# x loaded a second time with its axes exchanged and normed in place, scores scaled at the drain, and block 2's norm, the choices and the expert rows put in another order

## The chip, the core and the metric

One core of one Trainium2 chip runs the whole kernel. The metric is device time in microseconds (us). One profiled execution of the kernel before is read; its engines are PE (TensorE, with PEld for its weight loads), DVE (VectorE), ACT (ScalarE), POOL (GpSimd, which only issues indirect DMAs here) and SP (SyncE, which only issues DMAs).

## The reference

One layer on x, 512 tokens by 1024 features, all float32. What matters, cut down:

```python
hn = rmsnorm(x, mix_norm_w)                 # x * rsqrt(mean(x^2)) * w
z, xbc, dt_raw, q, k, v = split(hn @ w_in)
y = concat(ssd_branch(z, xbc, dt_raw), diff_attention(q, k, v))
x = x + y @ w_out
xn = rmsnorm(x, ffn_norm_w)
# PEER, 8 heads: scores of 2 x 128 keys, top 16 of each half, top 16 of their sums
h = gelu(xn . peer_u[idx]);  x = x + sum((g * h) * peer_v[idx])   # 128 experts a token, of 16384
```

In the attention a head has two score maps (queries and keys of 64 features, scale 64 ** -0.5), a softmax of each, and the value product of the first less lambda times the second.

## The kernel before, in words

Tokens lie in four blocks of 128. Blocks 0 and 1 are half 0, blocks 2 and 3 are half 1. `T8[:, half]` holds the operand of the projections with features on partitions: 8 chunks of 128 features by 256 tokens.

`work_order()` (L93) writes one list of steps, `ORDER`. PE, ACT and DVE each walk it and do their part of every step, in that order, so an engine that waits holds back all its later steps. Semaphores join them.

**Start.** SP loads x (four blocks), constants, `WDT`, `ROWS`, then the weight tiles of `w_in`, 2 MB each in two halves. ACT and DVE square and sum x (L877, L1108), `inverse_mean` and a root give the factor, L1115 writes the normed block to `Y`, PE turns it with 8 transposes a block (L597, 32 in all), and DVE drains the banks into `T8` with the norm's weight (L1101, two a block). Steps: x is one block of 128 channels of the convolution's input (8 logical products, L627), dt the 8 columns of dt (L743, both halves of the tokens), cv a convolution, acs, z, q, k, v, S1 to S3 (the SSD branch) follow.

**Attention**, blocks 0 and 1 (maps i = 0 to 7) and then blocks 2 and 3 (i = 8 to 15), written by `attention()`. Step A: PE scores (L701), DVE maximum and its scaled negative (L1372, L1375), ACT exponentials (L968). c: DVE joins the two maps (L1382). B: PE turns the map (L711), ACT copies it (L976). C: values (L723) into bank 2. N and n2: norm of a block, on DVE and ACT (L1387 to L1398, L985 to L991). T turns the normed block, R0 and R1 multiply it with `w_out` (L635), F and U norm and turn the sum, W and K (L807) give queries and scores of the keys. Between the maps lie fill products and, on DVE, rows.

**Expert layer.** Half 0 fetches its experts' rows: for a token's 128 experts one row of u (`ru`, L1431, 1.22 us of DVE) and one of v (`rv`, L1436, 1.28 us), each an indirect DMA of 512 KB issued by POOL (L1481) into one of 5 to 13 places (`RING`, and spaces in `BIG` while these are free). Half 1 goes densely over all 128 tiles of `u_t` and of v: step gl (L824) is one tile of u_t, 64 of them before the one-hot steps begin; r and y are DVE's choices of the top 16; sel turns the choices (PE L830), ACT copies them to `KT3` (L1056, L1059), oh builds one-hot matrices from them (DVE L1340, ACT), og multiplies them (PE L843), gm and gw multiply the gates into `HBUF` (L1452, L1456). The second 64 turns of the loop at L192 hold oh, gm, gl, og, gw and two or three rows each. Then come 128 tiles of v (L849) on PE and the rest of the rows on DVE, and `fin` (L1464) adds the two and stores.

The order of choices and rows among the first 64 gl steps is written by a cost loop: an item is put before gl j+1 while the costs spent are under a due time,

```python
while w < len(work) and spent < 3.44 * (j + 1) - 4:      # L186
```

where 3.44 us is one gl step. Scores of half 0's block 1 are stored to DRAM (`away`, L527) between the key load (L525) and the last tiles of `w_q`.

Of the kernel before, what the change touches and what calls it, by code (L numbers as in the profile page):

```python
# [92 lines left out]
def work_order():  # L93
# [87 lines left out]
    work += [first] + rows(2) + on("sel", 0) + rows(2) + on("oh", 0) + [second] + rows(3) + on("oh", 1) + [keys]  # L181
    work += rows(1) + on("ws", 3)
    spent, w = 0.0, 0
    for j in range(FIRSTJ):
        o += on("gl", j) if j else []
        while w < len(work) and spent < 3.44 * (j + 1) - 4:  # L186
            o.append(work[w])
            spent += cost[work[w][0]]
            w += 1
    o += work[w:]  # L190
    g = 0
    for k, j in enumerate(range(FIRSTJ, NKEY)):  # L192
        if 0 < g < NGRP - 1:
            o += on("oh", g + 1)
        if k >= 3:
# [6 lines left out]
        o += rows(2 + (k % 4 == 0))  # L202
# [11 lines left out]
def block_program(nc, x, w_in, w_out, w_q, keys_t, u, u_t, v, rows, ffn_w, cols, consts, out, away, x_kept):  # L214
    ctx = ExitStack()
    with ctx:
# [82 lines left out]
        LT = TMP[:, 0, 0:QKD]  # L299
        WC = sb("WC", [P, 8])  # L300
# [43 lines left out]
        ld_x = [sem(f"ld_x{i}") for i in range(NB)]  # L344
        ld_id, ld_par, ld_fw, ld_keys, ones_set = (sem(n) for n in ("ld_id", "ld_par", "ld_fw", "ld_keys", "ones_set"))
# [17 lines left out]
        chosen, g_raw, g_exp, idx_ready = (sem(n) for n in ("chosen", "g_raw", "g_exp", "idx_ready"))  # L363
        t_late, dense_keys, n_half, f_half = sem("t_late"), sem("dense_keys"), sem("n_half"), sem("f_half")
# [105 lines left out]
        def y_count(kind, b):  # L470
            return b + 1 if kind == 0 else NB + 1 + NORMS[("NF"[kind - 1], b)]

        def turned(b):

            return (t_done, 2 * NB + TURNS[("T", b)] + 1), (t_late, TURNS[("T", b)] + 1)

        def t_count(kind, b):
            return 2 * b if kind == 0 else 2 * NB + 2 * TURNS[("T", b)]
# [24 lines left out]
        def _(sp):  # L503
            for b in range(NB):
                sp.dma_start(X[:, b, :], x[b * P:(b + 1) * P, :]).then_inc(ld_x[b], 16)
                if b == 1:
                    sp.dma_start(CONST[:], consts[:, 0:2 * P]).then_inc(ld_id, 16)
            sp.dma_start(COLS[:], cols).then_inc(ld_par, 16)
# [4 lines left out]
            for n, (mat, c0) in enumerate(tiles):  # L513
                if n == 2:
                    sp.wait_ge(t_full, 2 * NB)
# [14 lines left out]
                for half in range(2):  # L530
                    s = (2 * n + half) % NHALFW
# [991 lines left out]
```

## Time and profile before

| | us |
|---|---|
| three runs | 1433.91, 1436.22, 1436.32 (median 1436.22) |
| the profiled execution | 1435.16 |
| its span, first to last instruction | 1433.4 |
| PE busy | 1376.7 (96%) |
| DVE busy | 1107.8 (77%) |
| ACT / POOL busy | 400.2 / 615.9 |
| moved by DMA | 466.12 MB, 325 GB/s in the mean |
| mean granted TensorE clock | 0.992 |

1.8 us of the execution's time lie outside the span. A busy PE is an engine with a matrix product in flight. Matrix products in float32 are two records each.

### The profile page before, as it was taken

How to read it: one execution, taken by the hardware profiler on the slowest of the kernel's cores; microseconds unless marked ns; L12 is line 12 of the kernel's file. 1: busy time of each engine (PE TensorE's matmuls, PEld its weight loads, DVE VectorE, ACT ScalarE, POOL GpSimd, SP SyncE). 2: the span in 40 equal slices, each digit the busy share in tenths (PEclk: the TensorE clock that was granted, in tenths of full speed). 3: DMA queues.
4: the chain of work that ended last, by engine and by line, in shares of the span. 5: the costliest groups of instructions: out<-in, count | busy, mean ns of one | idle time of the engine just before them, and what ended most of it. 6: DMA issues, size and time to landing. Idle time of an engine off the chain costs nothing.

```text
span 1433.4 us, 16343 instructions
## 1 busy us (share of the span) xinstructions
PE 1376.7 (96%) x5426; PEld 938.1 (65%) x5426; DVE 1107.8 (77%) x2587; ACT 400.2 (28%) x1097; POOL 615.9 (43%) x516
## 2 busy tenths in 40 slices
PE   7999999998999999999899999999999999999996
PEld 5756647566488888888799988885444444444442
DVE  2545446899799999998989889997877767776666
ACT  2423532334311121112666676662000000000000
POOL 0000001542745544432366565665366665564541
PEclk9999999999999999999999999999999999999998
DMA  6333345974999998988699999999899999999998
GB/s 219 126 118 124 118 144 177 358 275 153 403 366 400 394 345 297 376 304 284 235 394 389 383 367 367 371 375 392 337 411 410 409 410 409 409 409 409 409 409 322
DMA packets 140084, 466.12 MB, mean 325 GB/s; under 512 B 14561, under 2 KB 14945, under 8 KB 139489
## 3 DMA queue, kind: packets, MB, share of 16 engines
q0 software_dynamic: 73728, 268.47, 48.7%
q1 hardware_dynamic: 66272, 196.61, 36.4%
q8 instruction: 44, 0.72, 0.2%
q14 instruction: 40, 0.32, 0.1%
HBM read 461.09 MB, written 3.93 MB: 324 GB/s over the span
## 4 chain that ended last, share of the span: by engine, by line
PE 43%; DMA 29%; DVE 17%; issue 5%; POOL 3%; ACT 1%; SPq 0%; DVEq 0%; ACTq 0%
PE BANKS L824 15%; PE BANKS L635 9%; PE BANKS L849 9%; DMA UV<-v,IDX 8%; PE BANKS L627 7%; DMA UV<-u,IDX 7%; DMA BIG<-u,IDX 7%; DMA BIG<-v,IDX 5%; DVE X L1436 4%; POOL UV L1481 2%; DVE UV L1431 1%; DMA BIG<-w_q 1%; DVE BIG L1431 1%; DMA Y<-keys_t 1%; DVE BIG L1452 1%
## 5 line engine op out<-in xcount | busy, mean ns | idle before, releaser
L1481 POOL DMA_INDIRECT UV<-u,IDX x145 | 174.0, 1200 | 375.3 <-DVE IDX L1320 257.5
L1481 POOL DMA_INDIRECT UV<-v,IDX x166 | 210.2, 1266 | 188.0 <-DVE UV L1431 94.8
L1436 DVE SCALAR_TENSOR_TENSOR X<-UV,HG,X 128x1024 f32<-128x1024 f32 x166 | 213.0, 1283 | 40.7 <-DMA UV<-v,IDX 36.2
L824 PE MATMUL BANKS<-T 128*128 128x256 f32 x1024 | 229.1, 379 | 0.0
L849 PE MATMUL BANKS<-T,BIG 128*128 128x512 f32 x512 | 225.2, 592 | 1.8 <-DVE BIG L1452 1.8
L849 PE MATMUL BANKS<-Y,BIG 128*128 128x512 f32 x512 | 225.1, 592 | 0.0
L824 PE MATMUL BANKS<-T,Y 128*128 128x256 f32 x992 | 223.2, 381 | 0.0
L1431 DVE SCALAR_TENSOR_TENSOR UV<-UV,Y 128x1024 f32<-128x1024 f32 x145 | 176.5, 1223 | 46.4 <-DMA UV<-u,IDX 45.5
L824 PEld LDWEIGHTS BANKS<-T 128*128 128x128 f32 x1024 | 192.1, 190 | 24.8
L824 PEld LDWEIGHTS BANKS<-T,Y 128*128 128x128 f32 x992 | 187.0, 191 | 24.3
L1481 POOL DMA_INDIRECT BIG<-u,IDX x111 | 130.5, 1175 | 126.1 <-DVE BIG L1431 39.0
L849 PEld LDWEIGHTS BANKS<-T,BIG 128*128 128x128 f32 x512 | 97.1, 190 | 124.1 <-issue 121.2
L849 PEld LDWEIGHTS BANKS<-Y,BIG 128*128 128x128 f32 x512 | 97.3, 190 | 122.5 <-issue 122.5
L627 PE MATMUL BANKS<-T,BIG 128*128 128x256 f32 x768 | 173.8, 385 | 3.3 <-DVE T L1103 1.5
L635 PE MATMUL BANKS<-BIG,T 128*128 128x512 f32 x384 | 167.6, 593 | 0.6 <-DVE T L1103 0.6
L627 PEld LDWEIGHTS BANKS<-T,BIG 128*128 128x128 f32 x768 | 146.2, 193 | 26.4 <-issue 4.1
L1431 DVE SCALAR_TENSOR_TENSOR BIG<-BIG,Y 128x1024 f32<-128x1024 f32 x111 | 134.7, 1223 | 36.7 <-DMA BIG<-u,IDX 36.2
L1481 POOL DMA_INDIRECT BIG<-v,IDX x90 | 101.0, 1122 | 101.3 <-DVE BIG L1431 43.5
L1436 DVE SCALAR_TENSOR_TENSOR X<-BIG,HG,X 128x1024 f32<-128x1024 f32 x90 | 115.6, 1285 | 33.5 <-DMA BIG<-v,IDX 32.0
L635 PEld LDWEIGHTS BANKS<-BIG,T 128*128 128x128 f32 x384 | 72.0, 190 | 85.1 <-issue 84.9
L1040 ACT ACTIVATE BIG<-BANKS 128x256 f32<-128x256 f32 (+20 forms) x128 | 42.3, 330 | 185.9 <-PE BANKS L824 185.6
L1074 ACT ACTIVATE X<-X,KT 128x128 f32<-128x128 f32 x224 | 92.6, 485 | 0.0
(264 smaller groups left out, 1200.8 us busy)
## 6 DMA issues: line engine op xcount, KB each, us to landing
T<-u_t SPq DMA_DIRECT2D x64, 512.0 KB, 6.6
T<-v SPq DMA_DIRECT2D x64, 512.0 KB, 6.8
Y<-v SPq DMA_DIRECT2D x64, 512.0 KB, 6.8
Y<-u_t SPq DMA_DIRECT2D x62, 512.0 KB, 6.5
BIG<-w_in SPq DMA_DIRECT2D x24, 1024.0 KB, 7.4
BIG<-w_q SPq DMA_DIRECT2D x16, 1024.0 KB, 11.4
BIG<-w_out SPq DMA_DIRECT2D x8, 1024.0 KB, 7.3
UV<-v,IDX POOLq DMA_INDIRECT x166, 8.2
```

What stands on the lines that cost most here:

```text
L627: last = nc.tensor.matmul(bank[:, 0:HT], wt, T8[:, half, c, :], start=(c == 0), stop=(c == KC - 1))
L635: last = nc.tensor.matmul(bank[:, :], T8[:, b // 2, c, b % 2 * P:(b % 2 + 1) * P], wt, start=(c == 0), stop=(c == KC - 1))
L824: last = nc.tensor.matmul(PS[(i + 2) % 4][:, 0:HT], ub[:, c, :], T8[:, 1, c, :], start=(c == 0), stop=(c == KC - 1))
L849: last = nc.tensor.matmul(PS[4 + 2 * t + n][:, :], HBUF[:, j, t * P:(t + 1) * P], STREAM[j % NS][:, n * HALF:(n + 1) * HALF], start=(j == ...
L1040: last = nc.scalar.activation(HBUF[:, i, n:HT], bank[:, n:HT], ACT.Gelu)
L1074: last = nc.scalar.activation(ONEHOT[:, i % 2, 1, k, :], ONEHOT[:, i % 2, 1, k, :], ACT.Relu, bias=KT3[:, 2, t:t + 1], scale=KT3[:, 3, t:t ...
L1431: stt(row, row, 1.0, Y[:, n // 4, :], ALU.mult, ALU.mult, accum_out=acc).then_inc(used, 1)
L1436: stt(xb, row, HG[:, n % 2, i % UNIT:i % UNIT + 1], xb, ALU.mult, ALU.add).then_inc(used, 1)
L1452: tt(hb, hb, PS[4 + i % 4].rearrange("p (j t) -> p j t", t=NTOK)[:, 0:JS[i], :], ALU.mult)\
L1481: pool.indirect_dma_start(row_place(s), None, u if kind == "ru" else v, bass.IndirectOffsetOnAxis(IDX[:, b, c:c + 1], 0)).then_inc(row_in[ ...
```

## The change

It has these parts.

1. `x_t`, the same x with features on partitions, 8 KB in a row for each partition and half, is a new input, laid out on the host. SP loads it into `T8` (1 MB a half). `Y` gets no normed x, and the 32 transposes and 8 drains go. Instead DVE writes two 128x128 diagonals a half (`DIAG`), PE multiplies ones by them (`scale_map`, 2 products a half), which gives the factor of each token on every partition, and DVE multiplies each chunk in place (8 a half). The weight tile 0 is loaded ahead of x's blocks 2 and 3, and the first steps are reordered: x 0 and x 1, dt, x 2.
2. The scale of the scores goes to the drain of the queries (ACT), and the maximum is written negated.
3. Block 2's norm (N, n2) moves from map 12 to map 13, behind the exponentials of map 15, and T of block 2 behind map 15. Block 3's values go to bank 1, and W 8 to 15 all use bank 0.
4. y 1 is done at map 11, and one row moves from map 14 to behind R0 3.
5. The keys are loaded in two halves, the first as soon as block 2 is turned; `away` moves to tile 24 of u_t.
6. Order in the expert layer: the due time loses its "- 4", sel 0 moves ahead of two rows, and in the second 64 turns one row goes between oh and gm.

The diff, cut to its core:

```diff
-    o = many("x", 0, 1) + on("dt", 0) + many("x", 1, 2) + on("dt", 1) + many("cv", 0, 1)
-    for i in range(2, 8):
+    o = many("x", 0, 2) + on("dt", 0) + many("x", 2, 3) + on("dt", 1) + many("cv", 0, 2)
+    for i in range(3, 8):
...
-            ended = [i // DH - 1] if i > first and i % DH == 0 else []
+            ended = [0] if i == DH else []
...
+            late = [2] if i + 3 == NB * DH else []
+            for b in late:
+                out += on("N", b)
...
-            for b in ended:
+            for b in ended + late:
                 out += on("n2", b)
             then = after.get(i, [])
-            ahead = ended or i % 8 == 6
+            ahead = ended or i in (6, 14, 15)
...
-    between = {9: [first], 10: [second], 12: [keys]}
+    between = {9: [first], 10: [second], 11: [keys]}
...
-        after[i] = many("W", i + 1, min(i + 2, 16)) + (between[i] if i in between else rows({8: 4, 11: 1, 13: 3, 14: 4, 15: 0}[i]))
-        if i == 12:
-            after[i] += on("T", 2)
-    after[15] += on("N n2", 3) + rows(2) + on("R0", 2) + on("T", 3) + rows(4) + on("R0", 3) + rows(4) + on("R1 Q", 2)
+        after[i] = many("W", i + 1, min(i + 2, 16)) + (between[i] if i in between else rows({8: 4, 12: 1, 13: 3, 14: 3, 15: 0}[i]))
+    after[15] = on("T", 2)
+    after[15] += on("N n2", 3) + rows(2) + on("R0", 2) + on("T", 3) + rows(4) + on("R0", 3) + rows(5) + on("R1 Q", 2)
...
-    work += [first] + rows(2) + on("sel", 0) + rows(2) + on("oh", 0) + [second] + rows(3) + on("oh", 1) + [keys]
+    work += [first] + on("sel", 0) + rows(4) + on("oh", 0) + [second] + rows(3) + on("oh", 1) + [keys]
...
-        while w < len(work) and spent < 3.44 * (j + 1) - 4:
+        while w < len(work) and spent < 3.44 * (j + 1):
...
+        o += rows(1)
         if k >= 3:
             o += [("gm", n) for n in range(max(0, g - 3), g) if ("gm", n) not in o]
...
-        o += rows(2 + (k % 4 == 0))
+        o += rows(1 + (k % 4 == 0))
...
+        DIAG = TMP[:, 0, :].rearrange("p (b n) -> p b n", n=P)
...
+        v_bank = lambda b: 1 if b == NB - 1 else 2
+        w_bank = lambda i: 0 if PH <= i < 2 * PH else i % 2
...
+            load(0)
+            sp.dma_start(CONST[:], consts[:, 0:2 * P]).then_inc(ld_id, 16)
+            load(1)
+            sp.dma_start(COLS[:], cols).then_inc(ld_cols, 16)
+            sp.dma_start(T8[:, 0], x_t[:, 0]).then_inc(ld_t[0], 16)
+            load_tile(0, *tiles[0])
+            load(2)
+            load(3)
+            sp.dma_start(T8[:, 1], x_t[:, 1]).then_inc(ld_t[1], 16)
...
-                if n == 22:
-                    sp.wait_ge(ut_full, 2 * NB)
-                    sp.dma_start(KEYS, keys_t).then_inc(ld_keys, 16)
-                    sp.wait_ge(ks_done, 8)
-                    sp.dma_start(away, SCA1[:, 1:4, :].rearrange("p a n -> p (a n)")).then_inc(sc_away, 16)
+                if n in (22, 23):
+                    sp.wait_ge(ut_full, 2 * NB - 2 * (n == 22))
+                    part = slice((n - 22) * PH, (n - 21) * PH)
+                    sp.dma_start(KEYS[:, part, :], keys_t[:, part, :]).then_inc(ld_keys if n == 22 else ld_upper, 16)
...
+                if j == 24:
+                    sp.wait_ge(ks_done, 8)
+                    sp.dma_start(away, SCA1[:, 1:4, :].rearrange("p a n -> p (a n)")).then_inc(sc_away, 16)
...
+            def scale_map(half):
+                if half == 0:
+                    pe.wait_ge(ones_set, 1)
+                for b in range(2):
+                    pe.wait_ge(diag_ready, 2 * half + b + 1)
+                    last = nc.tensor.matmul(PS[half][:, b * P:(b + 1) * P], ONES, DIAG[:, 2 * half + b, :],
+                                            start=True, stop=True)
+                last.then_inc(scale_full, 1)
+            scale_map(0)
...
                     for half in range(2):
+                        if half:
+                            scale_map(1)
                         for c in range(KC):
+                            if half:
+                                pe.wait_ge(t_done, KC + c + 1)
...
+                for b in (2 * half, 2 * half + 1):
+                    ts(DIAG[:, b, :], IDENT, SS[:, b:b + 1], None, ALU.mult).then_inc(diag_ready, 1)
+                dve.wait_ge(ld_t[half], 16)
+                dve.wait_ge(scale_full, half + 1)
+                for c in range(KC):
+                    stt(T8[:, half, c, :], T8[:, half, c, :], COLS[:, V_MIX + c:V_MIX + c + 1], PS[half][:, 0:HT],
+                        ALU.mult, ALU.mult).then_inc(t_done, 1)
...
-                    link(nc.vector.reduce_max(MX[:, i % 2, :], maps[:, :, 0:P * (b + 1)], AXX))
                     if i >= 2:
                         dve.wait_ge(exp_done, 2 * (i - 1))
-                    ts(NMX[:, i % 2, :], MX[:, i % 2, :], -(QKD ** -0.5), None, ALU.mult).then_inc(mx_ready, 1)
+                    nc.vector.reduce_max(NMX[:, i % 2, :], maps[:, :, 0:P * (b + 1)], AXX, negate=True).then_inc(mx_ready, 1)
```

## Rows read from the trace of the kernel before

**Rows 1.** The page, busy time of each engine.

```profile
PE 1376.7 (96%) x5426; PEld 938.1 (65%) x5426; DVE 1107.8 (77%) x2587; ACT 400.2 (28%) x1097; POOL 615.9 (43%) x516
```

**Rows 2.** Stretches: length, busy of PE, PEld, DVE, ACT, POOL, clock, DMA share, GB/s.

```profile
300.00:360.00 60.00, 50.69 (x255) 38.17 (x252) 56.50 (x168) 26.10 (x77) 22.50 (x18) 0.97 0.61 215
360.00:396.00 36.00, 32.94 (x111) 16.94 (x111) 26.10 (x52) 13.28 (x27) 26.70 (x20) 1.00 1.03 403
...
500.00:650.00 150.00, 150.00 (x697) 132.05 (x696) 145.04 (x490) 22.40 (x50) 57.35 (x50) 1.00 0.90 332
...
650.00:700.00 50.00, 47.33 (x229) 41.53 (x227) 43.67 (x125) 18.60 (x47) 10.16 (x8) 1.00 0.68 228
...
703.00:985.00 282.00, 274.57 (x1477) 241.45 (x1475) 258.11 (x428) 191.15 (x620) 179.48 (x140) 1.00 1.00 376
985.00:1400.00 415.00, 415.00 (x967) 183.83 (x968) 289.44 (x535) 7.79 (x11) 232.83 (x204) 1.00 1.01 403
```

**Rows 3.** The end, in order of time: PE's last products and DVE's sum.

```profile
1412.55 7.03 PE L849 MATMUL BANKS<-Y,BIG 128*128 128x512 f32 x16
...
1427.70 2.48 DVE L1464 TENSOR_TENSOR X<-X,BANKS 128x512 f32<-128x512 f32 x4
```

**Rows 4.** The start on PE, in order of time: start, us, line, idle before.

```profile
8.74 3.65 PE L597 MATMUL BANKS<-CONST,Y 128*128 128x128 f32 x16 [8.74 <-DVE Y L1115]
...
16.83 4.80 PE L627 MATMUL BANKS<-T,BIG 128*128 128x256 f32 x16
21.56 7.07 PE L743 MATMUL BANKS<-T,BIG 128*8 128x256 f32 x32
28.57 3.72 PE L627 MATMUL BANKS<-T,BIG 128*128 128x256 f32 x16
...
55.08 13.98 PE L635 MATMUL BANKS<-BIG,T 128*128 128x512 f32 x32
```

**Rows 5.** Short stretches of the start (columns as in rows 2).

```profile
16.80:18.00 1.20, 1.20 (x5) 1.02 (x4) 1.20 (x3) 0.00 (x0) 0.00 (x0) 0.50 1.06 387
...
0.00:3.00 3.00, 0.00 (x0) 0.00 (x0) 0.20 (x2) 1.49 (x2) 0.20 (x4) 1.00 0.40 82
3.00:13.00 10.00, 3.65 (x16) 3.28 (x16) 4.75 (x12) 3.69 (x8) 0.00 (x0) 1.00 1.04 361
```

**Rows 6.** DVE's groups of the first 60 us, shapes kept apart: count, busy, mean ns.

```profile
L1164 DVE SCALAR_TENSOR_TENSOR BIG<-BIG,COLS 128x256 f32<-128x256 f32 x24 | 11.6, 484 | 0.9
L1101 DVE TENSOR_TENSOR T<-BANKS,COLS 128x512 f32<-128x512 f32 x8 | 5.0, 680 | 0.0
...
L1162 DVE TENSOR_SCALAR BIG<-BIG,COLS 128x256 f32<-128x256 f32 x8 | 2.8, 350 | 1.6 <-ACT BIG L889 1.5
```

**Rows 7.** A wait of 300 to 360 us, the negating instruction, ACT's part of a T.

```profile
PE BANKS L711 <- DVE BIG L1382: 6.2, 4, 1.8
...
L1375 DVE TENSOR_SCALAR NMX<-MX x16: 168/169/366, 126.2 to 348.1; 128x2 f32<-128x2 f32 x16
...
366.89 1.14 ACT L995 ACTIVATE T<-BANKS,WC 128x128 f32<-128x128 f32 x4 [4.14 <-PE BANKS L597]
```

**Rows 8.** Around sel 0 and the first one-hots, in order of time.

```profile
679.00 0.69 DVE L1340 TENSOR_TENSOR X<-CONST,KT 128x512 f32<-128x512 f32 x1 [5.05 <-ACT KT L1059]
...
677.78 0.38 PE L830 MATMUL BANKS<-CONST,BIG 128*128 128x128 f32 x2
...
700.96 1.26 PE L843 MATMUL BANKS<-X 128*128 128x128 f32 x8 [3.63 <-DVE X L1340]
...
698.23 1.73 POOL L1481 DMA_INDIRECT UV<-v,IDX  x1 [22.20 <-DVE UV L1431]
```

**Rows 9.** PE's wait for the keys, 400 to 450 us.

```profile
PE BANKS L807 <- DMA Y<-keys_t: 1.3, 1, 1.3
```

**Rows 10.** DVE's wait for u rows, 703 to 985 us, and PE's for one-hots.

```profile
DVE UV L1431 <- DMA UV<-u,IDX: 11.1, 16, 1.4
...
PE BANKS L843 <- DVE X L1340: 7.5, 5, 3.6
```

More of the change, by code:

```diff
@@ L211, in work_order, with block_program @@
     return o
-def block_program(nc, x, w_in, w_out, w_q, keys_t, u, u_t, v, rows, ffn_w, cols, consts, out, away, x_kept):
+def block_program(nc, x, x_t, w_in, w_out, w_q, keys_t, u, u_t, v, rows, ffn_w, cols, consts, out, away, x_kept):
     ctx = ExitStack()
@@ L503, in _, with load, load_tile @@
         def _(sp):
-            for b in range(NB):
+            def load(b):
                 sp.dma_start(X[:, b, :], x[b * P:(b + 1) * P, :]).then_inc(ld_x[b], 16)
-                if b == 1:
-                    sp.dma_start(CONST[:], consts[:, 0:2 * P]).then_inc(ld_id, 16)
-            sp.dma_start(COLS[:], cols).then_inc(ld_par, 16)
+            def load_tile(n, mat, c0):
+                for half in range(2):
+                    s = (2 * n + half) % NHALFW
+                    src = mat[half * 4 * P:(half + 1) * 4 * P, c0:c0 + HALF].rearrange("(c p) n -> p c n", p=P)
+                    sp.dma_start(W[:, s, :].rearrange("p (c n) -> p c n", n=HALF), src).then_inc(w_full[s], 16)
+            load(0)
[7 more added lines that the diff above has]
+            sp.dma_start(T8[:, 1], x_t[:, 1]).then_inc(ld_t[1], 16)
             sp.dma_start(WDT.rearrange("p (c n) -> p c n", n=NH),
@@ L579, in transpose_block @@
                 for c in range(2):
-                    if kind and c == 0:
+                    if c == 0:
                         pe.wait_ge((n_half, f_half)[kind - 1], b + 1)
@@ L615, in next_bank @@
                 return PS[4 + j % 4]
-            pe.wait_ge(ld_id, 16)
-            for b in range(NB):
-                transpose_block(0, b)
-            pe.wait_ge(t_done, NB)
+            def scale_map(half):
[7 more added lines that the diff above has]
+            scale_map(0)
             def channels(half, cb, n, bank, signal, halves=()):
                 for c in range(KC):
-                    if halves and c % 4 == 0:
-                        pe.wait_ge(*halves[c // 4])
+                    if len(halves) == KC or halves and c % 4 == 0:
+                        pe.wait_ge(*halves[c * len(halves) // KC])
                     wt = W[:, (n + c // 4) % NHALFW, (c % 4) * HALF + cb % 4 * P:(c % 4) * HALF + (cb % 4 + 1) * P]
@@ L719, in values @@
                     pe.wait_ge(y_free, 6 * (i // 8 + 1))
+                elif h == 0 and v_bank(b) == 2:
+                    pe.wait_ge(y_ready, y_count(1, b - 1))
                 elif h == 0:
-                    pe.wait_ge(y_ready, y_count(1, b - 1))
+                    bank_01(1, y_ready, y_count(1, b))
                 for kb in range(b + 1):
-                    last = nc.tensor.matmul(PS[2][:, h * P:(h + 1) * P], AT[:, kb * P:(kb + 1) * P],
+                    last = nc.tensor.matmul(PS[v_bank(b)][:, h * P:(h + 1) * P], AT[:, kb * P:(kb + 1) * P],
                                             V[:, kb, h * P:(h + 1) * P], start=(kb == 0), stop=(kb == b))
@@ L733, in _ @@
                     if half == 0:
-                        channels(0, cb, n, next_bank(), proj_full)
+                        channels(0, cb, n, next_bank(), proj_full, [(t_done, c + 1) for c in range(KC)] if cb == 0 else ())
                     else:
@@ L797, in _ @@
                         n = weights_in()
-                    channels(half, j, n, bank_01(j % 2, q2_done, i + 1), q2_full,
+                    channels(half, j, n, bank_01(w_bank(i), q2_done, i + 1), q2_full,
                              [(ut_done, 4 * half + 3 + c) for c in range(2)])
@@ L801, in _ @@
                     half, c, b = i // 8, i % 8 // 2, i % 2
-                    pe.wait_ge(ld_keys, 48 if half else 16 if c < 2 else 32)
+                    if half:
+                        pe.wait_ge(*((ld_keys, 48) if c < 2 else (ld_upper, 16)))
+                    else:
+                        pe.wait_ge(ld_keys, 16 if c < 2 else 32)
                     bank = bank_01(i % 2, ks_done, i + 1)
@@ L882, in _, with drain_bank @@
             job = [0]
-            def drain_bank(dst, func=ACT.Copy, view=None):
+            def drain_bank(dst, func=ACT.Copy, view=None, scale=1.0):
                 j = job[0]
@@ L1018, in _ @@
                     act.wait_ge(q2_full, i + 1)
[L1019 removed]
+                    nc.scalar.activation(Q2[:, q_at(i // (2 * PH), i % (2 * PH)), :], PS[w_bank(i)][:, 0:HT], ACT.Copy).then_inc(q2_done, 1)
                 elif step == "K":
@@ L1113, in _ @@
                 dve.wait_ge(rs_done, half + 1)
+                if half == 0:
+                    dve.wait_ge(ld_id, 16)
+                    dve.wait_ge(ld_cols, 16)
                 for b in (2 * half, 2 * half + 1):
[L1115 to L1123 removed]
+                    ts(DIAG[:, b, :], IDENT, SS[:, b:b + 1], None, ALU.mult).then_inc(diag_ready, 1)
[4 more added lines that the diff above has]
+                        ALU.mult, ALU.mult).then_inc(t_done, 1)
+            dve.wait_ge(ld_par, 48)
+            nc.vector.tensor_copy(WC[:, 0:4], COLS[:, V_SSD:V_SSD + 4])
+            link(ts(WC[:, 4:8], COLS[:, V_SUB:V_SUB + 1].broadcast_to([P, 4]), 1.0 - LAMBDA_INIT, None, ALU.mult))
             dt = DT[:, :, :].rearrange("p b h -> p (b h)")
@@ L1507 @@
     arrays = {
-        "x": f["x"][0], "w_in": f["w_in"][0], "w_out": f["w_out"][0], "w_q": f["peer_w_q"][0],
+        "x": f["x"][0], "x_t": f["x"][0].reshape(2, HT, KC, P).transpose(3, 0, 2, 1), "w_in": f["w_in"][0], "w_out": f["w_out"][0], "w_q": f["peer_w_q"][0],
         "keys_t": f["peer_sub_keys"][0].reshape(2 * PH, NKEY, P).transpose(2, 0, 1),
```

82 lines of the change are left out of this document (30 added, 52 removed).

## The prediction, made before the changed kernel was run

> **What bounds the kernel now.** The page's busy times come first [rows 1]: PE works for 1376.7 of 1433.4 us, so one is tempted to count PE's work alone. The stretches say where that is wrong [rows 2]. From 500 to 650 us PE has no idle time, but DVE is busy for 145.0 of 150 too, with DMA at 0.90. From 650 to 700 both have gaps and DMA falls to 0.68. From 703 to 985 DMA is at 1.00, from 985 to 1400 at 1.01 (403 GB/s). The end tells which of them counts [rows 3]: PE's last product ends at 1419.6, and DVE works on rows until 1427.7, when the final sum begins. So the end is set by the stream of rows: in the attention by the order of DVE's steps, up to 700 us by DVE, then by bytes. What brings that stream forward before 700 us, where DMA has air, arrives at the end; what only frees PE does not.
>
> So each part is asked one thing: by how much is DVE's place in the list earlier at 700 us?
>
> **The start.** PE begins x 0 at 16.83 us and is through x 0, dt and x 1 at 32.3 [rows 4], and is busy without a gap from there on; so this stage hands on what PE saves. Before x 0 lie 32 transposes, of which the first 16 already wait for DVE's normed x. All that goes. The new start of x 0 is set by a transfer: weight tile 0 now stands behind x's blocks 0 and 1 (1.05 MB), constants and columns (0.16), x_t's half 0 (1.05), and is 2.10 MB itself, 4.36 MB. The first 3 us move 0.25 MB, the next run at 361 GB/s [rows 5], so the tile is in at 3 + 4.11/0.361 = 14.4 us. Later transfers can mix in. From above: in the kernel before the tile stood behind 0.33 MB more and was in by 16.83, so here it is by 15.9. I take 14.8, nearer to the rate. DVE is ready by then: the chain to the diagonals is the old one to PE's first transpose (8.74), with a smaller last instruction. Its 8 new instructions a half are 128x256 with an operand in PSUM; the trace has that shape only with all operands in SBUF, 484 ns [rows 6], each there linked to the one before. The bounds are 0.35 us (L1162, which reads one tensor) and 0.68 (L1101, twice as wide, from PSUM); 0.48 is nearest, 3.9 us for 8, done by about 14.
>
> Then x 0 costs 4.80 us as before, not 3.72 as x 1, because the granted clock is 0.50 (1.2 GHz) at 16.8 to 18 us, after an interrupted start [rows 4, 5]; x 1 3.72; dt's first half 3.53 (half of 7.07); the second map, 2 products of 128 columns, 0.45; then PE waits for DVE's first chunk, one instruction and the handovers, 0.7; dt's second half 3.9, since DVE's 0.48 a chunk is over PE's 0.44. Sum 17.1 us, end at 31.9: **0.4 us earlier**. Bounds about that: the tile 0.4 earlier or 1.1 later, the clock 1.1 us for or against, DVE's chunks 1.0 for or 0.9 against (past their half's first, they run beside x 0 and only the second half shows): -3.1 to +2.5 in all, so a gain of -2.7 to +2.9. DVE's chain of dt starts some 2 us later, behind x 2, and the convolutions with it; the first to need them all, the SSD maps, stand behind z's products (13.98 us [rows 4]), which cover it; without that cover it would cost its 2 us.
>
> The Trainium skill, "TensorE: Matmul & The Clock Gate", Part 4, says that transposes do not count as work for the clock; the trace fits, since the clock fell to 0.50 behind them. By it nothing warm is lost with them, and the sum stays as it is; its Part 1 says that an idle TensorE sits at the lower clock, which makes the upper price (a slow x 1 too, 1.1 us) the likelier of the two ends.
>
> **Attention.** In blocks 0 and 1 fill products cover the chain; the missing instruction gives 0 to 0.5, I take 0.2. In blocks 2 and 3 DVE is busy for 56.5 of 60 us while PE idles for 9.3, 6.2 of it for the joined map [rows 2, 7]. There DVE sets the pace. L1375 goes, 8 times 0.17 us and about 0.03 of handover: 1.6. One row (1.22) moves behind R0 3, where DVE has ten idle us (26.1 busy of 36 in 360 to 396 us) and PE's R1 products cover it: 1.2; without that cover it comes back whole. The new place of the norm keeps its root's table load from between the exponentials and costs DVE nothing, as its instructions are the same. Against it: the turning of block 2 now stands ahead of the last values, and R0 2 uses the same bank as ACT's part of it, at most ACT's four drains, 1.14 us [rows 7], with the values' products beside them; I take 0.3. W 8 to 15 in one bank cost nothing: ACT's drain of a W stands in its list ahead of the copy that PE's values before the next W need. Sum **2.5 us**, bounds 0 and 3. The norm's gain or loss beyond that is in them.
>
> **Keys and queries, 396 to 465 us.** The earlier and smaller key load takes away PE's wait of 1.3 [rows 9], perhaps a little for w_q too, and SP no longer waits for half 0's scores ahead of w_q. But DVE is full there and waits for none of it. **0 at the end**; PE gets 1 to 3 us further ahead, and without DVE as the bound those would be the gain. `away` (0.75 MB) only moves to tile 24 of u_t; the tiles queued behind it on SP are four places deep.
>
> **The expert layer's order.** Here is the largest term. DVE stands still for 5.05 us, from 673.95 until 679.00, because oh 0 needs ACT's copy of sel 0, which PE begins at 677.78 [rows 8]. PE is not late with data: sel 0 stands behind gl 61 in its list, though the last thing it needs, y 15, stands before gl 56. Without the "- 4" and ahead of two rows, sel 0's due time is 4 + 2.47 = 6.5 us earlier, two gl steps: behind gl 59. It is then in at about 672 less what PE has gained, while DVE comes to oh 0 at 674 less its 3.1. The wait is gone but for 0.3 at most: **5.0 us**, bounds 0 and 5.05. POOL stands still there too, 22.20 us [rows 8], and DMA is at 0.68, so the rows can follow. At og 2 PE waited 3.63 for DVE [rows 8]; DVE is then 8 us earlier and PE 4 to 6, so that wait shrinks to 1 to 2. ACT's waits for rows to leave `BIG` get a gl step tighter; PE has four banks of 3.44 us ahead of it. The row between oh and gm fills a gap of DVE but rows are limited there by their transfers (DVE waits 11.1 us for u rows alone, DMA 1.00 [rows 2, 10]): 0, bounds -1 and +3.
>
> **Sum.** 0.4 + 0.2 + 2.5 + 5.0 = 8.1 us. From 703 us on the same bytes are to be moved at the same rate, so it is kept. Against the profiled execution, 1435.16, that gives 1427.1; this execution lies 1.1 under the median of 1436.22, and against that I predict 1428.1, rounded **1428.0**.
>
> **Rivals.**
> - *Only the early parts arrive.* The 5 us at oh 0 come back as another wait, at oh 2 (y 4 lies ahead of it) or for rows: the ring has 5 places then, and POOL waited for DVE. For it: DMA is at 1.00 from 703 on. Against: nothing holds DVE at 674 but sel 0. 1436.2 - 3.1 = 1433.1. Chance 0.19.
> - *The loop packs better too.* The row ahead of gm removes PE's waits for one-hots (3.9 us of the 7.5 beside the one at og 2) and some of DVE's for rows. Against: DMA has no air. About 4 us more, 1424.0. Chance 0.12.
> - *It doesn't matter.* If the last 730 us hang on bytes alone, with requests made early enough anyway, or tile 0 is late by the 3 us of its bound and the clock with it, little is left: 1435.5. Chance 0.06.
> - *Slower.* gm now stands behind a row of 1.28 us and, worse, behind that row's transfer; ACT's copies and its gelu of the next gl stand behind gm, and PE's gl and og behind those. The turn is 4.4 us (282 by 64) and PE has four banks, so it decides from the point where DVE lags PE by four turns less that row. PE waited already five times in the loop [rows 10]. Were 0.2 us lost in each of 64 turns, 12.8: 1428.0 + 12.8 = 1440.8. For it: both engines and DMA are nearly full there, so no slack takes it up. Against: gm's data lags its turn by one only. Chance 0.09.
>
> **How the numbers follow.** The forecast has 0.54. A measurement of this kernel can tell about 0.2%, 2.9 us, from no change. The forecast, the packing and half or so of the first rival lie beyond it: 0.54 + 0.12 + 0.10 = 0.76 faster; the rest of that rival and the third, 0.15 same; 0.09 slower. The range: downward the bounds of the start (+2) and a part of the packing, 1423.0; upward through the first rival with its own spread of 2, 1435.0. About 0.85 by these cases, and the terms' errors eat some of it.
>
> **What would show it.** PE's first product near 14.8 and the end of dt near 32; 4 map products, no L597 before 150 us; PE's waits for c in blocks 2 and 3 well under 6 us, and the first R0 of block 2 some 3 us earlier; no wait of DVE ahead of the first L1340, which stands near 671; DMA above 0.68 in 650 to 700; the v products starting near 977 and the last row's product near 1419. Wrong would be: x 0 later than 17 us, a wait of several us at L1340 or for rows near 690, or a start of the v products that keeps less than half of the lead at 671.

## The result and the profile after

The changed kernel took 1427.75 us in the median of five runs (1424.92 to 1429.75), the kernel before beside it 1436.32 (1433.91 to 1439.75): a ratio of 0.9941, 95% interval 0.9925 to 0.9957, so 8.6 us less (6 to 11). The forecast was 1428.0. Two later measurements of the same file, each on its own chip and beside the kernel before, gave 0.9951 (0.9932 to 0.9971) and 0.9964 (0.9937 to 0.9992). The three, weighted by their intervals, give 0.9948 with 0.0011 to either side: 7.5 us less. The forecast of 8.1 holds. Its composition does not, and most of what follows is about that.

The page after, busy times, to be held against [rows 1]:

```profile
PE 1370.9 (96%) x5402; PEld 934.7 (66%) x5402; DVE 1103.4 (77%) x2579; ACT 397.1 (28%) x1095; POOL 621.2 (44%) x516
```

PE has 24 records less (32 of transposes go, 8 of the two maps come), DVE 8 instructions less. Nothing of this tells where 8 us went; the stretches do, as in [rows 2] (length, busy of PE, PEld, DVE, ACT, POOL, clock, DMA share, GB/s):

```profile
300.00:360.00 60.00, 50.59 (x255) 37.75 (x252) 54.34 (x161) 25.38 (x79) 22.05 (x18) 0.97 0.60 214
360.00:396.00 36.00, 32.95 (x112) 17.06 (x111) 26.79 (x51) 11.32 (x22) 26.19 (x21) 1.00 1.03 403
...
500.00:650.00 150.00, 150.00 (x696) 132.05 (x695) 144.22 (x490) 22.40 (x50) 56.42 (x49) 1.00 0.89 337
650.00:700.00 50.00, 48.15 (x231) 42.45 (x230) 48.57 (x134) 19.12 (x49) 14.22 (x11) 0.97 0.71 243
...
703.00:985.00 282.00, 277.66 (x1484) 242.68 (x1483) 258.44 (x425) 187.18 (x614) 182.52 (x142) 1.00 1.00 383
985.00:1400.00 415.00, 415.00 (x968) 183.61 (x967) 289.24 (x533) 7.79 (x11) 236.08 (x202) 1.00 1.02 403
```

From 650 to 700 us DVE works 4.9 us more and DMA moves 243 GB/s for 228. From 703 to 985 the row moves too: 383 GB/s for 376, at the same DMA share of 1.00. In the attention DVE works 2.2 us less from 300 to 360 us and 0.7 us more from 360 to 396, where the moved row went; nothing else changes by more than 2 us.

A second reading is more exact: DVE's row products come in the same order in both kernels, so the start of the k-th can be subtracted from the start of the k-th before. The difference is called the lead below. The changed kernel is ahead by this much (row, its time before, lead in us): row 0 at 257 us, 0.1; row 48 at 397, 0.1; row 112 at 548, 0.0; row 144 at 648, -0.8; row 160 at 699, 4.3; row 208 at 793, 3.2; row 240 at 857, 5.3; row 256 at 891, 9.0; row 304 at 989, 8.0; row 511 at 1426, 7.9. So in this pair of executions nothing at all was gained before 650 us, 5.1 at sel 0, and 3.7 between 699 and 989.

The start on PE, in order of time ([rows 4] before):

```profile
9.23 1.19 PE L644 MATMUL BANKS<-BIG 128*128 128x128 f32 x4 [9.23 <-DVE BIG L1146]
14.93 8.58 PE L655 MATMUL BANKS<-T,BIG 128*128 128x256 f32 x32 [4.51 <-DMA BIG<-w_in]
23.44 3.62 PE L774 MATMUL BANKS<-T,BIG 128*8 128x256 f32 x16
26.99 0.71 PE L644 MATMUL BANKS<-BIG 128*128 128x128 f32 x4
28.35 3.62 PE L774 MATMUL BANKS<-T,BIG 128*8 128x256 f32 x16 [0.64 <-DVE T L1150]
31.90 3.72 PE L655 MATMUL BANKS<-T,BIG 128*128 128x256 f32 x16
```

x 0 begins at 14.93 (forecast 14.8), behind a wait for the weight tile, and x 0, x 1 and dt are through at 31.90 (forecast 31.9; the kernel before 32.22).

The attention, in order of time: the product R0 of block 2 and the turning of block 2 on DVE that it waits for; then a row of the sums of PE's waits, 300 to 360 us ([rows 7] before).

```profile
357.94 0.68 DVE L1131 TENSOR_TENSOR T<-BANKS,WC 128x512 f32<-128x512 f32 x1
...
358.77 7.11 PE L663 MATMUL BANKS<-BIG,T 128*128 128x512 f32 x16 [1.75 <-DVE T L1131]
```

```profile
PE BANKS L737 <- DVE BIG L1410: 7.1, 5, 2.0
```

R0 of block 2 began at 358.95 before, so it is 0.2 us earlier, not 3. PE's wait for the joined map, which was to shrink well under 6 us, is 7.1. Two rows of DVE, in order of time, say what came in place of its 2.2 us of work: a wait for map 15's scores and one for ACT's root. The stretch behind them (columns as above) has the reason of the first.

```profile
344.37 0.17 DVE L1400 MEMSET BANKS<- 64x128 f32 x1 [1.58 <-PE BANKS L727]
...
348.90 0.16 DVE L1423 TENSOR_TENSOR RS<-RS,NSQ 128x4 f32<-128x4 f32 x1 [0.87 <-ACT NSQ L1020]
```

```profile
343.00:345.00 2.00, 2.00 (x8) 0.83 (x5) 0.60 (x2) 0.00 (x0) 0.45 (x1) 0.50 0.00 0
```

PE was idle for 2.04 us ahead of the map and ran at a granted clock of 0.50 (1.2 GHz) from 343 to 345: its four score records took 2.08 us instead of 1.13. In the traces of experiments 4, 5 and 8 the clock does not fall there, and DVE's wait for these scores is 0.6 us; PE's wait ahead of R0 of block 2 is 1.75 in all three all the same, so that one doesn't come from the clock.

Sel 0 and the first one-hots ([rows 8] before):

```profile
668.35 0.38 PE L864 MATMUL BANKS<-CONST,BIG 128*128 128x128 f32 x2
...
674.68 0.68 DVE L1369 TENSOR_TENSOR X<-CONST,KT 128x512 f32<-128x512 f32 x1
...
696.65 1.69 PE L877 MATMUL BANKS<-X 128*128 128x128 f32 x8 [1.85 <-DVE X L1369]
```

PE begins sel 0 at 668.35 for 677.78; DVE's first one-hot has no wait in front of it; PE's wait at og 2 is 1.85 for 3.63, within the forecast's 1 to 2. These three are as promised. The place of the first one-hot is not: it stands at 674.68 for 679.00, where the forecast had 671. The 5 us of the wait are gone, but the 3.1 us that DVE should have brought along from the start and the attention are not there.

The loop, waits of DVE and PE from 703 to 985 us ([rows 10] before), the first v product before and after, and the end ([rows 3]):

```profile
DVE X L1464 <- DMA UV<-v,IDX: 13.5, 22, 1.9
DVE UV L1459 <- DMA UV<-u,IDX: 7.8, 11, 2.9
...
PE BANKS L877 <- issue: 3.7, 4, 1.8
PE BANKS L883 <- DVE BIG L1480: 0.5, 1, 0.5
```

```profile
977.92 3.60 PE L849 MATMUL BANKS<-T,BIG 128*128 128x512 f32 x8
```

```profile
969.85 3.67 PE L883 MATMUL BANKS<-T,BIG 128*128 128x512 f32 x8 [0.20 <-issue]
```

```profile
1407.82 2.74 PE L883 MATMUL BANKS<-Y,BIG 128*128 128x512 f32 x6
...
1418.38 1.28 DVE L1464 SCALAR_TENSOR_TENSOR X<-BIG,HG,X 128x1024 f32<-128x1024 f32 x1
1419.80 2.48 DVE L1492 TENSOR_TENSOR X<-X,BANKS 128x512 f32<-128x512 f32 x4
```

PE no longer waits for one-hots behind 703 us. A part comes back as a wait for nothing that the profile shows (3.7 us of "issue" for 1.7), so that PE idles for 4.3 us of the 282 instead of 7.4. DVE waits as long for rows as before (21.3 us for 21.5), yet begins 141 of them for 139. The v products start 8.1 us earlier. The forecast's "near 977" for them was no sign of a lead, since the kernel before begins them at 977.92; it had counted from 985, where its stretches end. The last row stands at 1418.38, near the promised 1419, and the final sum 7.9 us earlier.

### The profile page after: what moved, and what is told of

Same layout as the page of the kernel before. It is cut to its first block, busy times and chain, and to the rows that moved or that the text cites. A ratio compares the mean times of both kernels' runs of the same rounds, so it can differ in the third digit from the quotient of the medians.

```text
span 1425.8 us, 16284 instructions
## 1 busy us (share of the span) xinstructions
PE 1370.9 (96%) x5402; PEld 934.7 (66%) x5402; DVE 1103.4 (77%) x2579; ACT 397.1 (28%) x1095; POOL 621.2 (44%) x516
## 4 chain that ended last, share of the span: by engine, by line
DVE 35%; DMA 29%; PE 21%; issue 9%; POOL 5%; ACT 1%; SPq 0%; DVEq 0%; ACTq 0%
DMA UV<-v,IDX 10%; DVE X L1464 9%; DMA BIG<-u,IDX 9%; PE BANKS L663 9%; DMA BIG<-v,IDX 5%; PE BANKS L655 5%; PE BANKS L883 4%; DMA UV<-u,IDX 4%; POOL UV L1509 4%; DVE UV L1459 3%; DVE BIG L1459 2%; DVE BIG L1293 2%; DVE BIG L1285 2%; POOL BIG L1509 1%; DVE BIG L1287 1%
## 5 line engine op out<-in xcount | busy, mean ns | idle before, releaser
L1509 POOL DMA_INDIRECT UV<-v,IDX x168 | 213.7, 1272 | 149.1 <-DVE UV L1459 68.9
L1509 POOL DMA_INDIRECT BIG<-v,IDX x88 | 102.9, 1169 | 70.9 <-DVE BIG L1459 31.9
```

Of the source, the lines that this page charges most:

```text
L1509: pool.indirect_dma_start(row_place(s), None, u if kind == "ru" else v, bass.IndirectOffsetOnAxis(IDX[:, b, c:c + 1], 0)).then_inc(row_in[ ...
```

## The experiments

All ratios are to the kernel before, measured beside it on the same chip; "us" behind a ratio is (1 - ratio) times 1436. Single executions of one file spread widely (the kernel before from 1427.75 to 1443.45 in the first group), so verdicts go by the ratios, and the traces say where.

**1. Only sel 0 and the due time, in the kernel before.**

```
-    work += [first] + rows(2) + on("sel", 0) + rows(2) + on("oh", 0) + [second] + rows(3) + on("oh", 1) + [keys]
+    work += [first] + on("sel", 0) + rows(4) + on("oh", 0) + [second] + rows(3) + on("oh", 1) + [keys]
...
-        while w < len(work) and spent < 3.44 * (j + 1) - 4:
+        while w < len(work) and spent < 3.44 * (j + 1):
```

> The kernel before with sel 0 ahead of the rows and the due time without the minus 4, nothing else. Prediction's theory: the 5.05 us wait is gone and the end is 5.0 us earlier, 1431.3. Rival 1, the loop in its old order gives a part back (oh 2, rows not in): 1433 to 1436. Rival 2, without PE's 2.5 us of lead sel 0 is in only at 672 to 673 and DVE still waits 1 to 2 us: 1432 to 1433.

Measured: 1431.17, ratio 0.9968 (0.9948 to 0.9987), 4.6 us less (2 to 7). The wait at oh 0 is gone and the lead at row 160 grows by 5.2 (from 0.6 at row 144 to 5.8), but only 2.5 is left at row 304. So the term of 5.0 is right at its place, and the loop in its old order takes a part back in the trace: rival 1 in a small size.

**2. The expert layer's whole new order, in the kernel before**: experiment 1 and

```
+        o += rows(1)
         if k >= 3:
             o += [("gm", n) for n in range(max(0, g - 3), g) if ("gm", n) not in o]
...
-        o += rows(2 + (k % 4 == 0))
+        o += rows(1 + (k % 4 == 0))
```

> The kernel before with the whole new order of the expert layer: sel 0, the due time, and the row ahead of gm in each turn. Prediction's theory: 1431.3, as without the row. Rival 1, the row's place gives 4 to 5 us by itself: 1427, so nearly all of the change's gain. Rival 2, the loop gains only with the attention's and the keys' lead in front: 1431.

Measured: 1424.68, ratio 0.9922 (0.9894 to 0.9950); and a second time, on another chip:

> The kernel before with the whole new order of the expert layer (sel 0, due time, row ahead of gm) once more, beside the changed kernel on the same chip. Theory C (the order of the expert layer is all of the change's gain, and x's new path, the attention's part and the keys' bring nothing or cost 1 to 3 us): 0.992 to 0.995 of the kernel before, 0 to 4 us under the changed kernel. Prediction's theory: 3.1 us over the changed kernel.

Measured: 1431.78, ratio 0.9943 (0.9920 to 0.9966). Both weighted: 0.9935, with 0.0018 to either side, 9.4 us less. That is all of the change's gain (7.5), without x's new path, the attention and the keys. Rival 1 of the first expectation and theory C of the second hold; the forecast's 3.1 us on top are not there. That the changed kernel is slower than this part of itself isn't shown: the difference is 1.9 us, with 3 to either side.

**3. Only the row ahead of gm, in the kernel before.**

> The kernel before with the row ahead of gm in each turn of the loop, and nothing else. Prediction's theory (0 for the row's place): no difference from the kernel before. Theory B (the row's place is worth 6 us in the loop, from the pair b_sel and b_sel_loop): 0.9955 to 0.997 of the kernel before, with DVE's 5 us wait ahead of oh 0 still there and the lead made between 730 and 900 us.

Measured: 1434.47, ratio 0.9964 (0.9940 to 0.9989), 5.2 us less (2 to 9). Theory B. The wait at oh 0 is still there (4.9 us), the lead is 0.5 at row 160 and 6.0 at row 304. With experiment 1 it adds up: 4.6 + 5.2 = 9.8 for the measured 9.4 of both together.

**4. The changed kernel with that row put back behind gw**, and **5. with sel 0 and the due time put back** (the diffs above, reversed).

> The changed kernel with the one row of each turn of the loop put back behind gw (all else as changed). Prediction's theory, the row's place costs and gains nothing: 1427.8 us, and DVE's lead over the kernel before stays at about 3 us from row 176 (731 us) on plus what the bytes give. Rival 1, the place of the row gives the 4 to 5 us that the lead grows by between 825 and 891 us: 1432 to 1433, with the lead flat at 3 to 4 us from 731 us to the end. Rival 2, the growth comes from PE's greater lead (2.5 us at 462 us): 1427.8 again, and the growth stands in the trace at the same place.

Measured: 1435.87, ratio 1.0010 (0.9988 to 1.0033): all of the gain is gone. Against the changed kernel's 0.9948 the row's place is worth 8.9 us here, with 3.6 to either side. Its lead is 2.1 at row 160 and 2.7 at row 304.

> The changed kernel with sel 0 put back behind two rows and the due time back to minus 4. Prediction's theory: DVE waits again some 5 us ahead of oh 0 (a little more or less by PE's 2.5 us of lead: 2.5 to 5), and the end is 3 to 5 us later, 1431 to 1433. Rival, the loop takes the wait up since it is bound by bytes and its new order packs better: 1427.8 to 1429.

Measured: 1433.25, ratio 0.9988 (0.9966 to 1.0009), so 5.7 us worse than the changed kernel, with 3.5 to either side; DVE waits 6.0 us ahead of oh 0 again. The theory of the forecast, not its rival.

What the row's place does is seen in the stretch from 703 to 985 us, once for experiment 1 and once for experiment 3 (columns as above):

```profile
703.00:985.00 282.00, 272.38 (x1453) 236.52 (x1452) 254.79 (x424) 185.44 (x608) 177.61 (x139) 1.00 0.99 375
```

```profile
703.00:985.00 282.00, 279.63 (x1493) 246.45 (x1493) 261.07 (x430) 191.74 (x620) 190.24 (x143) 0.99 1.00 384
```

The three kernels without the row there moved 376, 375 and 378 GB/s in this stretch, the eleven with it 376 to 386, in the mean 381.2. The two ranges touch, since a fixed stretch of time catches each kernel at another place. Between the same two row products, 176 and 256, they don't: the time is 160.5, 161.3 and 158.0 us without the row there, and 154.6 to 157.4 with it. PE's waits for one-hots from 703 to 985 us were 3.9, 5.9 and 2.7 us without, and 0 to 2.1 with. DMA's share reads 0.99 or 1.00 in all of them. So the share was no sign of a full DMA: the rate rose at the same share, and behind 985 us, with another mix of transfers, the same 16 engines moved 403 GB/s at 1.01 [rows 2].

Why the row's place does this is argued, not shown. When PE stops for a one-hot, the tiles of u_t that it would free come later, and with the row there PE and DVE have more work done in the same time: PE 277.6 us in the mean for 274.0, DVE 259.3 for 256.7. But the same row also gives its own place free earlier in the turn, so that POOL can ask for the next one sooner. No run holds PE up without moving a row, or moves a row without touching PE's wait, so the two readings stay unseparated.

**6. The changed kernel again, twice.**

> The changed kernel once more, as the base for the others of this call. The first three experiments' runs of the kernel before had a median of 1434.3 with a spread of some 4 us from run to run, so this one should come out at 1426 to 1428. Theory A (the order of the expert layer alone carries the change, and x's new path costs 1 to 2 us since the old path ran at the full clock in other executions): the end of dt in its trace at 31.9 to 33.3 us, not earlier than in the kernel before with the clock at full (30.4 to 30.9).

Measured: 1431.68, ratio 0.9951 (0.9932 to 0.9971).

> The changed kernel, a third time, for the comparison with s_again and s_less on the same chip: 0.994 to 0.995 of the kernel before. The end of the first two steps of x and both halves of dt in its trace: 31.9 to 33.5 us.

Measured: 1432.70, ratio 0.9964 (0.9937 to 0.9992). They serve the start too. In every trace the moment can be read at which x 0, x 1 and both halves of dt are through. With the old path: 32.22 (the profile before), 30.41, 30.86, 32.16, 31.44, 31.71, 31.67, mean 31.5. With the new one: 31.90, 33.23, 33.40, 33.47, 32.04, 32.64, 33.65, mean 32.9. The new path is 1.4 us later. The old path stood at the late end of its own spread in the one profile that the forecast had: its x 0 took 4.80 us there, and 3.69, 3.69, 3.62, 3.62, 3.69 and 4.70 in the others. This is experiment 1's start, with the old path:

```profile
16.13 3.69 PE L627 MATMUL BANKS<-T,BIG 128*128 128x256 f32 x16
19.75 7.07 PE L743 MATMUL BANKS<-T,BIG 128*8 128x256 f32 x32
26.75 3.72 PE L627 MATMUL BANKS<-T,BIG 128*128 128x256 f32 x16
30.41 0.41 PE L750 MATMUL BANKS<-CONST,BIG 8*128 8x8 f32 x4
```

And the second repetition's, with the new one: x 0 and x 1 up to 21.1 us and behind it, then two stretches of 2 us.

```profile
15.16 6.21 PE L655 MATMUL BANKS<-T,BIG 128*128 128x256 f32 x14 [4.53 <-DMA BIG<-w_in]
```

```profile
21.21 4.05 PE L655 MATMUL BANKS<-T,BIG 128*128 128x256 f32 x18
```

```profile
16.00:18.00 2.00, 2.00 (x6) 1.56 (x6) 0.00 (x0) 1.50 (x3) 0.00 (x0) 1.00 1.04 426
...
22.00:24.00 2.00, 2.00 (x11) 1.76 (x10) 0.00 (x0) 0.23 (x1) 0.00 (x0) 1.00 1.06 388
```

x 0 and x 1 together took 8.58 to 10.20 us in the seven traces with the new path, where 7.3 is the full pace. PE comes to them after 4.5 to 5.3 us of idleness. Its first records begin 0.43 us apart, the later ones 0.22 us; 0.43 is also the distance in x 0 of the kernel before while its clock reads 0.50, so the first ones run at the lower clock. This lasts 2.7 to 6.1 us from the start of x 0. The column reads 1.00 there only because the trace has no record of the clock yet: its first one, at the full clock, comes within 0.3 us of the change of pace in each of the seven (21.1 us in this one).

With the old path PE does nothing but transposes before x 0. They begin 0.21 us apart. In four traces the clock rises among them, at 11.7 to 13.1 us, and the next ones begin 0.11 us apart; in two of these it falls to 0.50 again at 15 to 16 us and costs x 0 its 4.80 and 4.70 us. In the other three it rises at 17.1 to 17.8 us, as x 0 begins. So x 0 had the full clock in five of seven.

**7. The expert layer's order and x's new path**, in the kernel before.

> The kernel before with the expert layer's new order (as b_sel_loop, 1424.7) and x's new path as well: no transposes of x, the exchanged load, diagonals, and the step order x 0, x 1, dt 0, x 2. Prediction's theory: 0.4 us less, 1424.3. Theory A: 1.0 to 2.5 us later at the end of dt than b_sel_loop (30.86 us), all of which stays until 400 us, and 1426 to 1427 at the end, or 1424.7 if the rows' transfers take it up at 595 us.

Measured: 1431.39, ratio 0.9953 (0.9933 to 0.9973): 2.7 us worse than experiment 2, with 3.8 to either side. Theory A's direction, not resolved by the times; dt is through at 32.04, the earliest but one of the seven.

**8. The expert layer's order and the attention's part.**

```
-                    link(nc.vector.reduce_max(MX[:, i % 2, :], maps[:, :, 0:P * (b + 1)], AXX))
...
-                    ts(NMX[:, i % 2, :], MX[:, i % 2, :], -(QKD ** -0.5), None, ALU.mult).then_inc(mx_ready, 1)
+                    nc.vector.reduce_max(NMX[:, i % 2, :], maps[:, :, 0:P * (b + 1)], AXX, negate=True).then_inc(mx_ready, 1)
...
-        if i == 12:
-            after[i] += on("T", 2)
+    after[15] = on("T", 2)
```

with the norm, the banks and the moved row as in the change.

> The kernel before with the expert layer's new order (as b_sel_loop, 1424.7) and the attention's part of the change: no instruction for the negated maximum, block 2's norm and turning later, W in one bank, one row moved. Prediction's theory: 2.7 us less, 1422.0, with the first R0 of block 2 some 3 us earlier. Rival (read from the traces: DVE has 2.2 us less work from 300 to 360 us and stands still 2.2 us more, PE then waits 1.75 us for T of block 2): 1424.7, R0 of block 2 where it was.

Measured: 1433.97, ratio 0.9966 (0.9948 to 0.9984): 4.5 us worse than experiment 2, with 3.6 to either side. A gain of 2.5 is excluded. Between rows 16 and 48 (300 to 397 us) this kernel's lead grows by 1.1; in the kernels of experiments 2 and 3, whose attention is the old one, it grows by 1.6, 1.6 and 1.7, in that of experiment 1 it falls by 0.2. So the attention's part brings DVE nothing. That it costs as much as 4.5 is not borne out: with 2.7 for x it would leave 2.2 of the 7.5 us that the whole change has. Part of these two differences may be something else: the profiles of experiments 7, 8 and 9 all have a stop of several engines near 610 us, which the last section shows, and how many of the other executions have it isn't known.

**9. The changed kernel with the three rows of map 14 moved from ahead of T 2 to ahead of R0's sum of block 2.**

```
-        after[i] = many("W", i + 1, min(i + 2, 16)) + (between[i] if i in between else rows({8: 4, 12: 1, 13: 3, 14: 3, 15: 0}[i]))
+        after[i] = many("W", i + 1, min(i + 2, 16)) + (between[i] if i in between else rows({8: 4, 12: 1, 13: 3, 14: 0, 15: 0}[i]))
...
-    after[15] += on("N n2", 3) + rows(2) + on("R0", 2) + on("T", 3) + rows(4) + on("R0", 3) + rows(5) + on("R1 Q", 2)
+    after[15] += on("N n2", 3) + rows(5) + on("R0", 2) + on("T", 3) + rows(4) + on("R0", 3) + rows(5) + on("R1 Q", 2)
```

> The changed kernel with DVE's three rows of map 14 moved from ahead of T 2 to ahead of R0 2's sum, where DVE stands still for 2.6 us. If these three rows are what makes R0 2 late, PE's wait of 1.75 us ahead of R0 2 goes, R0 2 starts at about 357.1 instead of 358.8, and everything up to 465 us comes 1.5 us earlier; at the end 1.5 us less than the changed kernel if a lead of before 590 us arrives (the prediction's rule), nothing if the rows' transfers at 590 to 600 us take it up.

Measured: 1437.19, ratio 0.9983 (0.9967 to 0.9999), 4.6 us worse than the changed kernel beside it, with 3.6 to either side. PE's waits around the two R0, in this kernel:

```profile
358.98 7.10 PE L663 MATMUL BANKS<-BIG,T 128*128 128x512 f32 x16 [0.46 <-ACT T L1030]
...
369.16 20.84 PE L663 MATMUL BANKS<-BIG,T 128*128 128x512 f32 x48 [2.19 <-DVE T L1131]
```

The wait ahead of R0 2 fell from 1.75 to 0.46, but the wait ahead of the next R0 rose from 0.60 to 2.19, since the five rows now stand ahead of T 3. A miss as an improvement; as a test it says that the rows were what made R0 2 late, and that the time comes back one product later. Why the end is 4.6 us later isn't explained by it; in the profile, 4.9 us of DVE's lead go near 600 us, in two waits of 2.5 and 2.3 us for nothing that the profile shows.

**10. Experiment 2, with only those further parts that take something away**: the separate negation, the keys' load in halves, `away` behind tile 24.

> s_again and besides only the parts of the change that take something away without a new order: no separate instruction for the negated maximum (8 times 0.17 us of DVE), the second load of the keys in two halves of what is needed first, and the scores' copy to memory behind tile 24 of u_t. Left out: x's new path and the later norm and turning of block 2. If a lead from before 590 us arrives at the end: 1.5 us under s_again. If not (as the other runs say): the same as s_again. It would be the version that beats both kernels, or ties with s_again for it.

Measured: 1430.06, ratio 0.9931 (0.9904 to 0.9958), 9.9 us less than the kernel before. By the ratios of this group it is 1.7 us under experiment 2's kernel and 4.7 under the changed one, with 5 to either side; by the medians 1.7 and 2.6. It has the lowest median of its group of runs, but neither difference is resolved. In its profile PE is 2.2 us ahead at 462 us, and the end doesn't have that; the stop near 610 us lies between.

## Why the forecast was right, and where its steps were wrong

- *The bound.* "What brings that stream forward before 700 us ... arrives at the end" held for the 5 us at sel 0, within the noise of experiments 1 and 5. For what lies earlier it is doubtful. The changed kernel made no lead before 650 us, but experiment 2's first trace had one, 3.1 us at row 112 (548 us in the kernel before), and nothing of it was left at row 128: near 595 us DVE waited for rows in transfer. Waits in front of rows between 588 and 606 us, 0.6 to 4.8 us, stand in all eleven traces with the due time moved and in none of the three without (in three of the eleven the profile shows nothing that ended them). So with the new order DVE can be held there by the rows, where the forecast had DVE alone as the bound up to 700 us.
- *"From 703 us on the same bytes are to be moved at the same rate"* is the step that failed. The same bytes, but not the same rate: 376 GB/s with the old order of the loop and 381 in the mean with the new one. The reading behind it, "DMA has no air", took a share of 1.00 for a full DMA; but the share stayed at 0.99 to 1.00 while the rate rose, and the stretch behind it in [rows 2] had 403 GB/s at nearly the same share.
- *The row between oh and gm*, taken as 0 with bounds -1 and +3: experiments 2 (less experiment 1), 3 and 4 measured 4.8, 5.2 and 8.9, each with 3.5 to 4 to either side, together 6.3 with 2. Above the bound, and the largest term of all. The rival "the loop packs better too" named the mechanism and the sign, with about 4 us, and had 0.12. The slower rival, gm behind a row's transfer and ACT's copies behind gm, had the same place and did not come: PE's waits for one-hots shrank. Only single waits of PE for ACT, 3.1 and 2.2 us in experiments 7 and 9, look like it.
- *Sel 0*, 5.0: 4.6 (2 to 7) and 5.7 (2 to 9) in the times, 5.1 us of wait gone in the trace. Right, by the steps named.
- *The start*, 0.4 earlier: in the trace each term fitted within 0.3 us (14.93 for 14.8, 31.90 for 31.9, DVE's eight instructions of a half 0.40 us apart for 0.48), but the comparison was with one late draw of the old start. On the mean of seven against seven it is 1.4 later, a loss where a gain was put down, though within the bounds. The prediction's "nothing warm is lost with them" is the sentence that failed. It rested on the premise that transposes don't count as work for the clock, and on one trace in which the clock had fallen behind them. The seven traces with the old path speak against both: the clock rose with nothing but transposes before it, and x 0 had the full clock in five. What came in place of the transposes was idleness. The Trainium skill, "TensorE: Matmul & The Clock Gate", Part 1, says that an idle TensorE sits at the lower clock, and the traces agree: 0.43 us from record to record behind 4.5 us of idleness. On transposes the Trainium skill's Part 4 of the same page, which the prediction cites, and these seven traces differ, and the traces decide here. The slow x 1 of the forecast's bound didn't come, since the clock was full by then in all seven; x 0 alone took 5.0 to 6.6 us up to the start of x 1, for the forecast's 4.80.
- *The attention*, 2.5 and 0.2: 0 in the trace. The work did leave DVE (2.2 us). What was late next was not named: block 2's norm between c 14 and c 15, with the wait for ACT's root (0.87); map 15's scores (1.58, of which about 1 for the lower clock, since the wait is 0.6 without it); and the turning behind three rows of DVE, which holds up R0 (1.75). "Costs DVE nothing, as its instructions are the same" was the failed sentence: the instructions were the same, the wait in front of them was new.
- *Keys and queries*, 0 at the end with PE 1 to 3 us further ahead. PE is 2.5 us ahead at its first gl step, 459.36 us for 461.89, but that isn't shown to be this part's doing. In the six other traces with the keys in two halves PE stands between 2.7 us behind and 2.2 ahead there, and experiment 2's first trace, which has the old load, is 2.5 ahead as well. Only the wait for the keys is gone: 0.2 to 2.4 us in the seven traces with the old load, none in the six of the changed kernel and its variants, 0.7 in experiment 10. The 2.5 is a draw like the start's.
- So two terms were too high by 2.7 and 1.8 us and one too low by about 6, and the sum came out because they offset each other: the total was met by luck, the 5 us of sel 0 by reasoning. The terms as measured (5 at sel 0, 6.3 in the loop, -1.4 at the start) add up to 9.9, more than the 7.5 of the whole. Each of the first two has 2 us or more to either side, so the 2.4 between can be noise, or a cost of the attention's part (experiment 8); that stays open.

## What to carry to other kernels

A DMA share near 1 says that the engines always had something, not that they moved what they can: look at the GB/s of the stretch too, and at the waits of the engines that free its buffers, before writing "no air". Before a stage is compared with the trace of before, ask how much that stage varies between executions of one file; here the first 30 us vary by 1.8 us with the old path and by 1.8 with the new. The same goes for a lead read late in one pair of traces, as at 462 us. And for work taken from an engine, write down the wait that the next instruction on it then meets: a step moved between two dependent ones brings its wait along.

## What the runs showed of the hardware

- A clock of 1.00 early in a trace can stand for no record at all. With the new path it reads 1.00 while the records of x 0 begin 0.43 us apart, as they do where it reads 0.50 in the kernel before; at the trace's first clock record they go to 0.22 us (17.9 to 21.1 us in the seven traces). The distance from record to record tells the clock where the column has nothing.
- Transposes alone went along with a rise to the full clock: in experiment 1's trace it reads full from 12.1 us on, before any product.
- Around 605 to 620 us, where POOL's row requests come in a burst, five of the fourteen traces have a stop of several engines with nothing to wait for that the profile shows. Experiment 10's is one:

```profile
605.00:610.00 5.00, 2.85 (x10) 1.61 (x8) 3.58 (x11) 0.38 (x1) 4.09 (x4) 0.91 1.02 408
610.00:615.00 5.00, 2.64 (x5) 1.15 (x5) 2.80 (x7) 0.13 (x1) 1.89 (x3) 0.50 1.03 409
```

```profile
PE BANKS L831 <- issue: 4.2, 5, 1.6
...
DVE BIG L1306 <- remote: 2.6, 1, 2.6
```

PE falls 9.5 us behind there, a part of it at a granted clock of 0.50 that follows its pauses, and DVE 4.3; DMA's share is 1.02 to 1.03 at the time. The same stop is in experiments 7, 8 and 9 and in the second repetition of the changed kernel; the other nine, the first repetition and the two kernels' own profiles among them, have none of this size. The five profiled executions that have it took 2.7 to 10.2 us more than the median of their kernel's, the other nine from 4.7 less to 2.1 more, so the stop is a part of the spread from execution to execution. Its several us are more than the start's whole effect, so one profile of each kernel can't settle such an effect. What sets it off stays open.
